# Projection chunks of a hybrid decoder in another order, with the gated mixer beneath later chunks

## What is computed

```python
h = rmsnorm(x, norm1_g)
z = h @ w_in                       # 1024 x 2328: u 512, v 512, q 512, kv_c, kv_s, kv_w 256 each, gate 24
u = gelu(u); vf = gelu(v)
vn = (vf - mean(vf)) * rsqrt(var(vf) + EPS) * ln_g + ln_b      # per head of 64
out = u * (tril(w_s) @ vn + b_s)                               # per 128 rows: the gated mixer, o_a
o_a = rmsnorm(out, out_norm_a)
# then compress(k, pe, w1, b1, w2): windows of 32 rows of K and V of 8 paged sequences and the prompt
hid = gelu(blk @ w1 + b1); k_c = hid @ w2                      # blk = rows + pe
# attention of samples and prompt (compressed, selected, window), projection w_out, SwiGLU FFN, final rmsnorm
```

## Time and profile before

| what | value |
|---|---|
| median of 3 runs | 1785.28 us (1785.13 to 1788.56) |
| profiled execution | 1777.76 us, span 1775.9 us |
| PE busy | 1627.3 us |
| VectorE, ScalarE, GpSimd busy | 813.1, 499.2, 492.4 us |
| mean granted TensorE clock | 0.962 |

### The profile page before, as it was taken

One profiled execution on the slowest core, in us unless ns is written; L12 is line 12 of the kernel. 1 busy time (PEld: TensorE's weight loads), 2 busy tenths in 40 slices (PEclk: granted clock), 3 DMA queues, 4 the chain that ended last, 5 costly groups with the idle time before them and its releaser, 6 DMA issues.

```text
span 1775.9 us, 26693 instructions
## 1 busy us (share of the span) xinstructions
PE 1627.3 (92%) x9867; PEld 1405.0 (79%) x9867; DVE 813.1 (46%) x1503; ACT 499.2 (28%) x1038; POOL 492.4 (28%) x491
## 2 busy tenths in 40 slices
PE   6899997589767999999899999999999999999995
PEld 6799997578436767777577988998899889988994
DVE  5010852243223789998335144334433443344337
ACT  5112312222111666767324221112111211121112
POOL 4322531442301554445112122112211211121112
PEclk9999998599887999999999999999999999999998
DMA  6321000622722000000500211211121111111102
GB/s 213 147 65 48 25 31 2 159 68 73 211 64 66 7 4 5 7 1 1 178 1 0 72 36 50 57 35 35 50 57 35 35 56 50 35 35 55 52 12 96
DMA packets 97897, 99.04 MB, mean 56 GB/s; under 512 B 6777, under 2 KB 83162, under 8 KB 97722
## 3 DMA queue, kind: packets, MB, share of 16 engines
q1 hardware_dynamic: 74906, 75.43, 13.8%
q0 software_dynamic: 4880, 12.96, 2.5%
q10 hardware_dynamic: 18032, 9.59, 2.0%
HBM read 90.81 MB, written 11.34 MB: 58 GB/s over the span
## 4 chain that ended last, share of the span: by engine, by line
PE 81%; DVE 6%; issue 3%; ACT 3%; POOL 3%; DMA 2%; ACTq 1%; POOLq 1%; SPq 0%; DVEq 0%
PE bankpair L2201 9%; PE bankpair L2203 9%; PE bankpair L2202 9%; PE bankpair L2228 5%; PE bankpair L2229 5%; PE bankpair L2230 5%; PE bankpair L359 4%; PE bankpair L360 4%; PE bankpair L363 4%; PE bankpair L969 3%; PE bankpair L1741 3%; PE bankpair L1821 2%; PE bankpair L1822 2%; PE bankpair L1710 2%; PE bankpair L1823 2%
## 5 line engine op out<-in xcount | busy, mean ns | idle before, releaser
L2201 PE MATMUL bankpair<-h2T_high,w_high 128*128 128x344 f32 x1056 | 337.6, 320 | 0.0
L2203 PE MATMUL bankpair<-h2T_high,w_low 128*128 128x344 f32 x1056 | 337.1, 319 | 0.0
L2202 PE MATMUL bankpair<-h2T_low,w_high 128*128 128x344 f32 x1056 | 337.1, 319 | 0.0
L2252 POOL TENSOR_TENSOR w_low<-work,w_high 128x1024 fp32r<-128x1024 f32 x44 | 105.3, 2418 | 566.1 <-ACT w_high L2247 566.0
L2331 DVE TENSOR_TENSOR x_all<-x_all,bankpair 128x512 f32<-128x512 f32 (+1 forms) x396 | 251.6, 683 | 1.2
L2317 DVE TENSOR_TENSOR kT_space<-kT_space,bankpair 128x344 f32<-128x344 f32 x66 | 33.9, 513 | 451.4 <-ACT kT_space L2265 451.4
L2265 ACT ACTIVATE kT_space<-bankpair 128x344 f32<-128x344 f32 x66 | 30.2, 458 | 623.8 <-PE bankpair L2203 623.7
L359 PE MATMUL bankpair<-win_high,h_high 128*128 128x256 f32 (+3 forms) x648 | 190.9, 295 | 13.0 <-POOL win_low L524 7.2
L2201 PEld LDWEIGHTS bankpair<-h2T_high,w_high 128*128 128x128 f32 x1056 | 198.6, 188 | 2.9
L2202 PEld LDWEIGHTS bankpair<-h2T_low,w_high 128*128 128x128 f32 x1056 | 198.1, 188 | 0.9
L2203 PEld LDWEIGHTS bankpair<-h2T_high,w_low 128*128 128x128 f32 x1056 | 198.4, 188 | 0.0
(11 more groups left out here) (310 smaller groups left out, 2816.7 us busy)
## 6 DMA issues: line engine op xcount, KB each, us to landing
work<-in_w_gate SPq DMA_DIRECT2D x22, 512.0 KB, 5.0
work<-in_w_up SPq DMA_DIRECT2D x22, 512.0 KB, 6.3
work<-in_w_down SPq DMA_DIRECT2D x22, 512.0 KB, 3.8
x_all<-in_x_prompt SPq DMA_DIRECT2D x15, 512.0 KB, 11.0
work<-in_w_in SPq DMA_DIRECT2D x7, 1024.0 KB, 5.1
work<-in_cache_kv_cmp SPq DMA_DIRECT2D x32, 128.0 KB, 2.7
work<-in_cache_kv_cmp POOLq DMA_DIRECT2D x32, 128.0 KB, 2.8
work<-in_cache_kv_slc POOLq DMA_DIRECT2D x32, 128.0 KB, 3.7
```

The source lines that it names most:

```text
L2201: pe.matmul(out, wh, high, start=(k == 0), stop=False)
L2202: pe.matmul(out, wh, low, start=False, stop=False)
L2203: ins = pe.matmul(out, wl, high, start=False, stop=(k == KD - 1))
L2252: pool.tensor_tensor(w_low[s][x], w_raw[s][x], w_high[s][x].bitcast(F32), ALU.subtract).then_inc(gu_low, 1)
```

## The change

It reorders stage 1 and the beginning of stage 2. What is computed stays.

- The chunks come in the order v, v, kv compress, u, u, kv selected, kv window with gates, q, q. The mixer's v work runs beneath chunks 1 and 2, `mix` beneath the u chunks 3 and 4, `turn_oa` beneath chunks 4 and 5.
- Beginning: ScalarE squares x tiles 0 and 1 ahead of all rounding, GpSimd makes both roots ahead of the low parts, PE turns tiles 0 and 1 ahead of the first projection, and the turned tiles alternate between two PSUM pairs.
- Buffers of the beginning and of the kv and u tiles lie in `kT_space` and `q_all`; `kvst` has 4 slots instead of 3.
- SP loads chunks 2, 3 and 4 ahead of the copy of the window state. The raw rows of sequence 0 are loaded behind `oaT`, those of sequence 1 behind the eighth chunk, w1 by SP behind the ninth; sequence 0 is sorted during the last chunk.
- The gate's Tanh comes in chunk 7; two semaphores for the split of K and V become one.

```diff
-    CH = [(1536, 256), (1792, 256), (2048, 280), (1024, 256), (1280, 256), (512, 256), (768, 256), (0, 256), (256, 256)]
+    CH = [(512, 256), (768, 256), (1536, 256), (0, 256), (256, 256), (1792, 256), (2048, 280), (1024, 256), (1280, 256)]
+    V_CH, U_CH, KV_CH, Q_CH = (0, 1), (3, 4), (2, 5, 6), (7, 8)
...
-            load_w_in(sp, 2)
+            for c in (2, 3, 4):
+                load_w_in(sp, c)
...
         turn_h(0)
+        turn_h(1)
         for t in range(XT):
             project(0, t)
             if t + 2 < XT:
                 turn_h(t + 2)
...
+        for hf, c in enumerate(U_CH):
             for t in range(XT):
                 project(c, t)
                 if t >= 1:
-                    turn_k((c - 1) * NT + t - 1)
-        for c in (3, 4, 5, 6):
+                    mix(hf, t - 1)
+                if hf == 1 and t >= 4:
+                    turn_oa(t - 4)
...
         square_x(act, 0)
-        for piece in range(2):
+        square_x(act, 1)
+        for piece in range(len(FIRST)):
             round_first(act, piece)
-        square_x(act, 1)
-        round_first(act, 2)
         take_hT(act, 0)
+        take_hT(act, 1)
         square_x(act, 2)
         for t in range(XT):
-            if t + 1 < XT:
-                take_hT(act, t + 1)
+            if t + 2 < XT:
+                take_hT(act, t + 2)
             if t + 3 < XT:
                 square_x(act, t + 3)
             take_z(act, 0, t)
-            if t == 5:
+            if t == 4:
                 round_w_in(act, 1)
...
         inv_x(0)
-        for piece in range(2):
-            low_first(piece)
         inv_x(1)
-        low_first(2)
-        inv_x(2)
-        for t in range(XT):
-            if t + 3 < XT:
-                inv_x(t + 3)
-            store_kv(0, t)
-            if t == 7:
+        for piece in range(len(FIRST)):
+            low_first(piece)
+        for t in range(2, XT):
+            inv_x(t)
+            if t == 6:
                 low_w_in(pool, 1)
...
-        act.wait_ge(z_ready, XT * NC)
...
+    def stage2_sync(sp):
+        sp.wait_ge(const_in, ALL_CONST)
+        sp.wait_ge(oaT_ready, XT)
+        load_raw(sp, 0, 0, raw_ready)
+        load_cmp_small(sp)
+        sp.wait_ge(z_ready, XT * (NC - 1))
+        load_raw(sp, 1, 0, raw_ready)
+        sp.wait_ge(z_ready, XT * NC)
+        load_w_cmp(sp)
```

More of the change, by code:

```diff
@@ L463, in stage1_scalar @@
             take_z(act, 0, t)
-            if t == 5:
+            if t == 4:
                 round_w_in(act, 1)
-        for c in range(1, 5):
+        for c in range(1, NC):
             for t in range(XT):
                 take_z(act, c, t)
-                if t == 3:
-                    round_w_in(act, c + 1)
[L471 to L504, removed]
+                if 0 <= zn(c - 1, t) - 2 < 2 * XT:
+                    square_v(act, zn(c - 1, t) - 2)
@@ new lines, in stage1_scalar @@
+                q = zn(c - 4, t)
+                if 0 <= q - 2 < XT:
+                    square_oa(act, q - 2)
+                if 0 <= q - 5 < XT:
+                    take_oaT(act, q - 5)
+                if t == 3 and c + 1 < NC:
+                    round_w_in(act, c + 1)
+                if c == 7 and t == 1:
+                    act.wait_ge(gate_raw, XT + 1)
+                    act.activation(gate[:, :, :], gate[:, :, :], ACT.Tanh, scale=0.5).then_inc(gate_tanh, 1)
+                if c == 8 and t == 5:
+                    sort_odd(act, 0)
@@ new lines, in square_oa, with take_oaT @@
+    def square_oa(act, t):
+        n = rows(t)
+        act.wait_ge(oa_ready, mixer(1, t) + 1)
+        if t >= 1:
+            act.wait_ge(oa_squared, t)
+        act.activation(sq_oa[0:n, :], v_rows_of(t)[0:n, :], ACT.Square, accum_out=ssa[0:n, t:t + 1]).then_inc(oa_squared, 1)
+    def take_oaT(act, t):
+        n = rows(t)
+        act.wait_ge(oa_turned, t + 1)
+        act.activation(oaT[:, :, P * t:P * t + n], pb(4 + t % 2).rearrange("p (k n) -> p k n", k=4)[:, :, 0:n], ACT.Copy)\
+           .then_inc(oaT_ready, 1)
@@ new lines, in inv_oa @@
+        def inv_oa(t):
+            n = rows(t)
+            pool.wait_ge(oa_squared, t + 1)
+            inv_rms(pool, chain.link, ssa[0:n, t:t + 1], ra[0:n, t:t + 1], 512).then_inc(oa_inv, 1)
+        inv_x(0)
+        inv_x(1)
+        for piece in range(len(FIRST)):
[3 more added lines that the diff above has]
+            if t == 6:
+                low_w_in(pool, 1)
+        for m in range(7):
+            inv_v(m)
+            if m == 2:
+                low_w_in(pool, 2)
@@ new lines, in stage1_pool @@
+        for t in range(XT):
+            inv_v(7 + t)
+            store_kv(0, t)
+            if t == 4:
+                low_w_in(pool, 3)
+        for m in (16, 17):
+            inv_v(m)
+        store_v(NT - 1)
+        store_v(NT)
+        low_w_in(pool, 4)
+        for t in range(XT):
+            inv_oa(t)
+            if t == 2:
+                low_w_in(pool, 5)
+        for b in (1, 2):
+            for t in range(XT):
+                store_kv(b, t)
+                if t == 4:
+                    low_w_in(pool, KV_CH[b] + 1)
```

311 lines of the change are left out of this document (155 added, 156 removed).

## The result

The changed kernel takes 1766.95 us (median of 4 runs, 1765.01 to 1769.51) against 1785.2 (1783.86 to 1788.56): a ratio of 0.990, 95% interval 0.988 to 0.992, 18.2 us less. 1755.7 was forecast, with 1738 to 1773 as the range. The profiled execution took 1766.52 us, its span is 1764.7.

A forecast was written before the change was run, and what follows sets the result against it. TensorE, busy 92% of 1775.9 us, was taken as the bound, so gains lie where it idles or runs slow. 7.7 + 21.9 = 29.6 us won gave 1748.2 profiled, 1755.7 as median; own range 1742 to 1770, widened to 1738 to 1773.

The forecast's parts named there:

- The chain of the beginning: Chunk 0: turn, copy, square, root and scaling take 5.5 us a tile instead of 3.7; chunk 1 starts at 70.
- rival 1: Chunk 0 isn't slowed and keeps 3.7 us a tile; chunk 1 starts near 50, 1735 us in all; chance 0.12.
- Chunks 1 to 8: Projection chunks after the first: 228.7 us plus 2.6 of waiting at the third mix, ending at 301.3.
- T: The end of the last projection, put at 301.3 against 308.98 before.
- From T to the first hidden sums: The stretch from last projection to first hidden sums: 37.5 us claimed against 59.4 before.
- the second term: Gain between the last projection and the first hidden sums: 21.9 us, range 18 to 28.
- I put it at T+9.5: Start of stage 2: both w1, 2 MB, land 9.5 us behind the last projection.
- rival 2: After the last projection: w1 and neighbours land at T+18, sums run cold, the second term shrinks to 11, 1767 us; chance 0.10.
- The second size: The bias sums ahead of the first hidden sums: 10.5 us, between 7.2 and 12.
- Behind it nothing changes: After the first hidden sums, the four further groups and all later stages move as a block.
- the prediction's own sign of being wrong: Among its signs of being wrong: later stages change their length by over 5 us.
- both terms: Gains up to the last projection, 7.7 us (1 to 14), and from there to the first hidden sums, 21.9 (18 to 28).

The follow-up runs named there:

- e2: The changed kernel with ScalarE squaring x one tile further ahead, as far as in the kernel before: 1759.46 us.
- e3: The changed kernel with x squared one tile further ahead and GpSimd's low half of chunk 1 behind all inverse roots: 1748.55 us.
- e8: The changed kernel with raw rows of sequences 0 and 1 loaded, and sequence 0 sorted, behind the last projection, w1 between them in SP's queue: 1781.11 us.
- e4: The changed kernel with SP and GpSimd waiting until w1 has landed before loading `kaug` and the raw rows of sequences 2 and onward: 1757.31 us.
- e9: The changed kernel with GpSimd loading `kaug` behind the raw rows of sequence 4 instead of first: 1761.06 us.
- e10: The changed kernel with 512 KB of unused x rows on 128 partitions loaded in place of `kaug`, itself loaded behind sequence 4's raw rows: 1760.72 us.
- e7: The changed kernel with ScalarE instead of SP issuing the w1 loads, so SP's raw rows of sequence 2 went out earlier: 1768.85 us.
- e13: The changed kernel with GpSimd loading its half of the raw rows of sequence 2 first and `kaug` behind it: 1769.36 us.
- e1: The changed kernel with GpSimd making the low half of chunk 1 behind all inverse roots: 1767.99 us.
- e12: The changed kernel with the edits of e3, e9 and e5 together: 1729.44 us.
- e5: The changed kernel with bias sums and first hidden sums cut in two, K first, waiting for V's w1 only then: 1762.57 us.

## Why the prediction was right, and where it was not

**The chain of the beginning: right.** It put the third turn at 20.4, the period at 5.5, the seventh and eighth turns at 42.4 and 54.6; the trace has 20.36, 5.48, 42.28 and 54.40. e2 and e3 show that the late square and the low half between the roots are the causes, and that rival 1 (the beginning isn't slowed) stood 18 us away: 1748.55 is its kernel. Chunk 1 was put at 70, of which 3 us were for the clock. ScalarE took its first tile at 70.6, so it started near 67.8, 0.9 us behind the 66.9 that the chain gives without the clock. It was 1.00 throughout the loop (24 to 46) and low only around the long gap (0.61 from 52 to 62). The rule of the Trainium skill that spoke against it, that frequent short idles make the clock go back and forth ("TensorE: Matmul & The Clock Gate", A second HAM failure mode: psum-queue depth-cycling), is not borne out here: with idles of 1.2 us every 5.5 us the clock stayed at 1.00.

**Chunks 1 to 8: right.** 231.3 us with the third mix were predicted. The third mix waited 3.15 us (2.6), PE waited for low halves 0.3 us in sum, and T came at 301.19 (301.3). The start came about 2 us earlier than predicted and the chunks took about 2 us more; the two errors cancel.

**From T to the first hidden sums: the raw rows were right, two sizes were not.** 37.5 us were predicted, 50.3 measured. That the second term rests on the early raw rows is shown by e8. The step that failed is "I put it at T+9.5" for the landing of w1. It came at T+19.6, which is rival 2's T+18. The 9.5 us are right for w1 without `kaug` at T (9.7 and 10.1 in e4 and e9). The prediction took the 7.2 us of the earlier trace rows as w1's price, but that row comes from a kernel in which `kaug` was issued 25 us behind w1. The prediction names `kaug` among the neighbours, but the 2.3 us that it adds to the row are all that issue and neighbours get. By e10, about half of the 10.1 us that are missing is the shape of `kaug` (4.9), and the other half is bytes (4.6 for 1 MB), as rival 2 had it; with `kaug` there, though, taking 512 KB away gave nothing (e7, e13). The second size is the bias sums, 10.5 predicted, 13.8 measured. They ran wholly at 0.50, also where PE had waited only 4.3 us for w1 (e4). In numbers: 10.1 us of landing, 3.3 of bias sums and 0.4 of hidden sums too little, 1.0 of seams too much, 12.8 together.

**Behind it nothing changes: right for the medians.** 16.8 us won at the activation, 18.2 in the medians. The 5.6 us that the profiled spans lose again stand at places where the granted clock differs in one execution and the other. That this is chance is argued, not shown. By the prediction's own sign of being wrong, later stages that change by over 5 us, these two executions speak against it (5.6 us); by the medians the later stages gave 1.4 us more.

**Sum.** 29.6 predicted: 7.7 and 21.9. The trace gives 7.8 and 9.0, the medians 18.2. The second term, 9.0, lies far outside its own 18 to 28. Even the lower bounds of both terms, 1 and 18, make more than the 18.2 us measured; only the 3 us between runs let 1766.95 into the forecast's 1742 to 1770. That the number lies in the range is luck as far as the second term goes. What happened to the second term is rival 2's mechanism (w1 late, sums cold), which was given 0.10 and forecast 1767.

## What to carry to other kernels

When a change moves a transfer, cost it also as a neighbour: what lands beside it, on how many partitions and with how long rows, and who waits for that; a duration read from a trace holds only for the neighbours it had there. When a loop has two late links, remove both in one kernel before judging either, since alone they won 9.1 and 1.2 us of its end and together 18.8. Where PE waits for two loads to do two sums, let it begin with the first, and look at what the clock was while it waited.

## What the runs showed of the hardware that was not expected

- A load of 528 KB onto 33 partitions, 16 KB on each, beside a 2 MB load held the DMA engines to 165 to 173 GB/s at a share of 0.91 to 0.96; a load of 512 KB onto 128 partitions, 4 KB on each, in its place left 230 GB/s at 0.91 (e10).
- A scaling of only 8 rows by 1024 took 5.51 us on VectorE beside a GpSimd low half of 4.49 us, against 1.28 us for 128 rows without it (e1).
- The bias matmuls, 128x1 with a 128x128 weight load each, are a stretch in which PE counts as busy and yet the granted clock falls: in e12 PE is busy without a break from 290 to 312, the clock is 1.00 at 302 to 304, and 0.50 at 308 to 312; between them lie 32 of these matmuls (304.66 to 309.15). It had come back to 1.00 in the hidden sums of K. e5 shows the same, 0.93 from 334 to 338 and 0.50 from 338 to 344, with no idle time between.
